# Token gather of a mixture-of-experts loop: the 0/1 matrix made the stationary operand, an eviction and transposes added, and the gather issued four weight chunks sooner

## What is computed

```python
def moe_swiglu(u, w_router, w_gate, w_up, w_down):
    logits = jnp.dot(t, w_router, preferred_element_type=jnp.float32)
    top_logit, top_idx = lax.top_k(logits, TOP_K)
    top_w = jax.nn.softmax(top_logit, axis=-1)
    gate = jnp.einsum('tk,tke->te', top_w, jax.nn.one_hot(top_idx, N_EXPERTS, ...)).astype(u.dtype)
    for e in range(N_EXPERTS):
        out = out + gate[:, e:e + 1] * swiglu(t, w_gate[e], w_up[e], w_down[e])
```

## Time and profile before

| | us |
|---|---|
| median of 3 runs | 1728.83 |
| lowest and highest | 1723.35, 1729.32 |
| the profiled execution's own time | 1729.09 |
| its span, from the first to the last instruction | 1727.3 |
| TensorE busy | 1595.1 |
| VectorE busy | 1303.5 |
| ScalarE busy | 1018.5 |

### The profile page before, as it was taken

One profiled execution on the slowest core, in us unless ns is written; L12 is line 12 of the kernel. 1 busy time (PEld: TensorE's weight loads), 2 busy tenths in 40 slices (PEclk: granted clock), 3 DMA queues, 4 the chain that ended last, 5 costly groups with the idle time before them and its releaser, 6 DMA issues.

```text
span 1727.3 us, 21466 instructions
## 1 busy us (share of the span) xinstructions
PE 1595.1 (92%) x8127; PEld 1346.3 (78%) x8127; DVE 1303.5 (75%) x1112; ACT 1018.5 (59%) x853; POOL 14.4 (1%) x35
## 2 busy tenths in 40 slices
PE   5996799998799777999999999999999999999985
PEld 5976688886697666888888888888888888888864
DVE  5986443544598654888988888888889888988863
ACT  4536243333454533767677767767677776777642
POOL 3000000000000000000000000000000000000000
PEclk9996799998899876999999999999999999999987
DMA  8430355553344033999999999999999999999930
GB/s 247 147 122 25 105 178 188 194 171 122 104 142 158 25 104 107 362 380 328 371 372 330 370 375 329 372 342 358 374 345 356 374 341 358 377 336 363 376 133 24
DMA packets 203166, 439.70 MB, mean 255 GB/s; under 512 B 12072, under 2 KB 31088, under 8 KB 203120
## 3 DMA queue, kind: packets, MB, share of 16 engines
q1 hardware_dynamic: 197040, 437.32, 71.7%
q10 hardware_dynamic: 6080, 1.74, 0.5%
HBM read 437.98 MB, written 1.05 MB: 254 GB/s over the span
## 4 chain that ended last, share of the span: by engine, by line
PE 85%; DVE 10%; ACT 3%; issue 1%; ACTq 0%; POOL 0%; DVEq 0%; POOLq 0%
PE bank L1177 25%; PE bank L1179 25%; PE bank L1178 25%; PE bank L1441 2%; DVE wlo L748 2%; PE bank L1472 1%; PE bank L1172 1%; PE bank L1247 1%; DVE uTl L798 1%; DVE scores L898 1%; PE bank L1311 1%; ACT work L497 1%; PE bank L1454 1%; PE bank L1455 1%; DVE work L793 0%
## 5 line engine op out<-in xcount | busy, mean ns | idle before, releaser
L748 DVE TENSOR_TENSOR wlo<-raw,whi 128x2048 fp32r<-128x2048 f32 x415 | 935.2, 2287 | 131.2 <-ACT whi L667 94.1
L667 ACT ACTIVATE whi<-raw 128x2048 fp32r<-128x2048 f32 x341 | 633.3, 1910 | 25.6 <-DMA raw<-in_w_exp_down_dram 14.4
L1177 PE MATMUL bank<-whi,uTh 128*128 128x512 f32 (+1 forms) x1312 | 520.9, 397 | 18.0 <-DVE uTl L798 17.0
L1179 PE MATMUL bank<-whi,uTl 128*128 128x512 f32 (+1 forms) x1312 | 513.3, 391 | 0.0
L1178 PE MATMUL bank<-wlo,uTh 128*128 128x512 f32 (+1 forms) x1312 | 512.8, 391 | 0.0
L1177 PEld LDWEIGHTS bank<-whi,uTh 128*128 128x128 f32 x1312 | 250.0, 191 | 70.4 <-DVE uTl L798 14.7
L1179 PEld LDWEIGHTS bank<-whi,uTl 128*128 128x128 f32 x1312 | 249.7, 190 | 52.8
L1178 PEld LDWEIGHTS bank<-wlo,uTh 128*128 128x128 f32 x1312 | 250.3, 191 | 49.5
L1177 PE MATMUL bank<-whi,hTr 128*128 128x512 f32 x552 | 218.1, 395 | 7.0 <-DVE hTr L964 4.4
L1178 PE MATMUL bank<-wlo,hTr 128*128 128x512 f32 x552 | 217.0, 393 | 0.0
L1179 PE MATMUL bank<-whi,hTr 128*128 128x512 f32 x552 | 216.8, 393 | 0.0
(11 more groups left out here) (212 smaller groups left out, 1158.2 us busy)
## 6 DMA issues: line engine op xcount, KB each, us to landing
raw<-in_w_exp_gate_dram SPq DMA_DIRECT2D x112, 1024.0 KB, 5.2
raw<-in_w_exp_up_dram SPq DMA_DIRECT2D x112, 1024.0 KB, 5.2
raw<-in_w_exp_down_dram SPq DMA_DIRECT2D x112, 1024.0 KB, 5.0
raw<-in_w_in_dram SPq DMA_DIRECT2D x28, 1024.0 KB, 5.4
raw<-in_w_ffn_gate_dram SPq DMA_DIRECT2D x11, 1024.0 KB, 5.0
raw<-in_w_ffn_up_dram SPq DMA_DIRECT2D x11, 1024.0 KB, 5.1
raw<-in_w_ffn_down_dram SPq DMA_DIRECT2D x11, 1024.0 KB, 4.8
raw<-in_w_out_dram SPq DMA_DIRECT2D x8, 1024.0 KB, 5.0
```

The source lines that it names most:

```text
L667: nc.scalar.activation(whi[:, s % SPLIT, :], raw[:, s % RAW, :], ACT.Copy).then_inc(hi_a, 1)
L748: return V.tensor_tensor(wlo[:, n % RAW, :], raw[:, n % RAW, :], whi[:, n % SPLIT, :].bitcast(F32), ALU.subtract).then_inc(lo_ready, 1)
L1177: T.matmul(o, sth, mvh, start=start, stop=False)
L1179: return T.matmul(o, stl, mvh, start=False, stop=stop)
```

## The change

The stationary operand of the gather becomes a tile of `sel`, the moving one 512 columns of the tokens' rows. High and low parts are added into the same bank, so that a bank holds 512 features of the 128 gathered tokens, places on partitions: 8 matmuls instead of 32, into banks 1 and 3. ScalarE evicts both banks to a new region `ug` (`tokens_out`). TensorE transposes `ug` in eight blocks of 128 into banks 7 and 1 (`gathered`), ScalarE copies the high parts from there, and VectorE, which before copied the low parts, now subtracts the high parts from the banks.

The order: the selection moves from chunk 35 to chunk 20, the gather matmuls from chunk 39 to chunk 35, with a wait for the hidden row of round 5. Behind chunk 39 stand the eight transposes and then the turn of round 6. Ahead of the loop, for the first item, the two parts follow each other.

```diff
+        ug = region(2560, D)
@@ ScalarE
+            def tokens_out(i, q):
+                act.wait_ge(gath, i * 2 + (q + 1))
+                nc.scalar.activation(ug[:, q * NC:(q + 1) * NC], bank(GATHER_BANKS[q]), ACT.Copy).then_inc(ug_ready, 1)
             def tokens_hi(i, q):
-                act.wait_ge(gath_hi, i * 2 + (q + 1))
-                nc.scalar.activation(uTeh[:, 4 * q:4 * q + 4, :], bank(GATHER_HI[q], 4, P), ACT.Copy).then_inc(euh_ready, 1)
+                act.wait_ge(gath_T, i * 2 + (q + 1))
+                nc.scalar.activation(uTeh[:, 4 * q:4 * q + 4, :], bank(TOKEN_BANKS[q], 4, P), ACT.Copy).then_inc(euh_ready, 1)
@@ ScalarE, in the loop, ahead of the weight copy of the chunk
+                    if n == GATHER_AT:
+                        for q in range(2):
+                            tokens_out(i + 1, q)
@@ VectorE
             def tokens_lo(i, q):
-                dve.wait_ge(gath_lo, i * 2 + (q + 1))
-                V.tensor_copy(uTel[:, 4 * q:4 * q + 4, :], bank(GATHER_LO[q], 4, P)).then_inc(eul_ready, 1)
+                s = slice(4 * q, 4 * q + 4)
+                dve.wait_ge(euh_ready, i * 2 + (q + 1))
+                V.tensor_tensor(uTel[:, s, :], bank(TOKEN_BANKS[q], 4, P), uTeh[:, s, :].bitcast(F32), ALU.subtract).then_inc(eul_ready, 1)
@@ TensorE
-            def gather(i, q, source, to, gathered):
+            def gather(i):
                 pe.wait_ge(sel_ready, i * 2 + 2)
-                for c in range(4):
+                for q in range(2):
                     for t in range(TT):
-                        k = 4 * q + c
-                        last = T.matmul(bank(to[q], 4, P)[:, c, :], source[:, t, k * P:(k + 1) * P], sel[:, t, :],
-                                        start=t == 0, stop=t == 1)
-                last.then_inc(gathered, 1)
+                        T.matmul(bank(GATHER_BANKS[q]), sel[:, t, :], unh[:, t, q * NC:(q + 1) * NC], start=t == 0, stop=False)
+                        last = T.matmul(bank(GATHER_BANKS[q]), sel[:, t, :], unl[:, t, q * NC:(q + 1) * NC], start=False, stop=t == 1)
+                    last.then_inc(gath, 1)
+            def gathered(i):
+                for q in range(2):
+                    pe.wait_ge(ug_ready, i * 2 + (q + 1))
+                    for c in range(4):
+                        last = T.transpose(bank(TOKEN_BANKS[q], 4, P)[:, c, :], ug[:, (4 * q + c) * P:(4 * q + c + 1) * P], ident[:, :])
+                    last.then_inc(gath_T, 1)
@@ TensorE, behind a chunk
                     if n == LAST_UP:
                         pe.wait_ge(comb_ready, i + 2)
-                        for q in range(2):
-                            gather(i + 1, q, unh, GATHER_HI, gath_hi)
+                        gathered(i + 1)
                         turn(r)
-                        for q in range(2):
-                            gather(i + 1, q, unl, GATHER_LO, gath_lo)
+                    if n == GATHER_AT:
+                        pe.wait_ge(exh_ready, i * EXR + (EXR - 1))
+                        gather(i + 1)
@@
-SELECT_AT = LAST_UP - 4
-GATHER_HI = [1, 7]
-GATHER_LO = [3, 0]
+SELECT_AT = 20
+GATHER_AT = LAST_UP - 4
+GATHER_BANKS = [1, 3]
+TOKEN_BANKS = [7, 1]
```

More of the change, by code:

```diff
@@ L318, in trunk @@
         rlog, rdiff, rexp, sel_count, ranks, table_ready = (sem(n) for n in ("rlog", "rdiff", "rexp", "sel_count", "ranks", "table_ready"))
-        sel_ready, gath_hi, gath_lo, euh_ready, eul_ready, comb_ps, comb_ready = (sem(n) for n in (
-            "sel_ready", "gath_hi", "gath_lo", "euh_ready", "eul_ready", "comb_ps", "comb_ready"))
+        sel_ready, gath, ug_ready, gath_T, euh_ready, eul_ready, comb_ps, comb_ready = (sem(n) for n in (
+            "sel_ready", "gath", "ug_ready", "gath_T", "euh_ready", "eul_ready", "comb_ps", "comb_ready"))
         exsil, exh_ready, exT_ps, exT_hi, exT_ready = (sem(n) for n in ("exsil", "exh_ready", "exT_ps", "exT_hi", "exT_ready"))
@@ L693, in _ @@
             for q in range(2):
+                tokens_out(0, q)
+            for q in range(2):
                 tokens_hi(0, q)
@@ L1457, in _ @@
             pe.wait_ge(unl_ready, TT)
-            for q in range(2):
-                gather(0, q, unh, GATHER_HI, gath_hi)
-            for q in range(2):
-                gather(0, q, unl, GATHER_LO, gath_lo)
+            gather(0)
+            gathered(0)
             with pe.Fori(0, n_items) as i:
```

## The result

| | before | after |
|---|---|---|
| median, us | 1726.33 (4 runs) | 1741.38 (4 runs) |
| lowest to highest | 1723.35 to 1729.32 | 1737.58 to 1744.53 |
| the profiled execution, its span | 1729.09, 1727.3 | 1737.58, 1735.8 |
| mean granted clock | 0.949 | 0.953 |

The ratio of the times is 1.0093, with a 95% interval from 1.0069 to 1.0117: the change makes the kernel 0.9% slower, about 15 us. The forecast was 1744, from 1736 to 1753.

A forecast was written before the change was run, and what follows sets the result against it. TensorE was taken to bound the expert loop. Eight item ends at +11.4 us, the first item at -1.0 and clock falls at +5.0 gave +15.4 on 1729.1 us: 1744, range 1736 to 1753.

The forecast's parts named there:

- The bound: Expert loop: TensorE, busy for all 983 us, sets the time, although the DMA engines have a share of 0.99.
- The work: TensorE per item: 3.5 us of gather removed, 1.86 of gather and 0.87 of transposes added; 0.75 us shorter by work alone.
- Chunk 35: Moved gather between two chunks: 1.86 us of uncovered TensorE time per item; hidden row then ready to start at T' + 0.57.
- T': Moment in the changed kernel when an item's last up chunk's matmuls are issued; forecast as 912.27 in the item shown.
- The item's end: After the last up chunk: TensorE idles 0.4, then 1.6 to 1.7 us; first down product 3.50 us on; item +1.43 us.
- First item: Gather ahead of the loop, at half clock: gains 1.4 us at most, some lost again; -1.0 us taken.
- longer time at half clock: Behind the first item's gather: expected to lose some of its gain of at most 1.4 us, leaving -1.0.
- The clock: Idle time at item ends lowers TensorE's granted clock: 0 to 8 falls, 0 to 13 us; three taken, +5.0 us.
- The price of one fall: Cost of one drop to half clock, read from eight matmuls taking 3.46 us instead of 1.81: 1.65 us.
- the second rival: Clock falls in every item, if transposes do not keep TensorE awake: +23.6 us, 1752.7; chance 0.14.
- VectorE in time: Item end: hidden row at T' + 0.2, turn follows transposes at once; +1.10 us per item, +7.8 in all, 1736.9; chance 0.11.
- Faster: Item-end stall is hidden and only the work counts: -7.0 us, 1722; chance 0.05.

The follow-up runs named there:

- the version with the other order: Changed kernel with round 6's up chunks ahead of round 5's down chunks, two turned-row buffers, transposes and last turn moved; ratio 0.9937, median 1716.26 us.
- The exchange of two lines in the kernel before: Kernel before with the sixteen low-part gather matmuls ahead of the last turn instead of behind it; ratio 1.0111.
- the filler: Changed kernel with seven extra 512-column matmuls behind an item's last turn, results overwritten; ratio 1.0038.
- the late transposes: Changed kernel with the eight transposes behind chunk 40 instead of ahead of the last turn; ratio 1.0201.
- 0.9 us more in each item: Changed kernel with four more 512-column matmuls behind chunk 12, results overwritten; ratio 1.0113.

## Why the prediction was right, and what was off

**The bound.** TensorE is the bound in the loop, and the DMA share of 0.99 was not a second one: the version with the other order went 0.8 us an item below the kernel before.

**The work.** 0.75 us less per item was forecast; the version without waits shows 0.8.

**Chunk 35.** The gather there took 1.8 us of TensorE, uncovered. The evictions stood at 0.90 and 1.81 behind the activation (forecast 0.96 and 1.87). The hidden row came at T' + 0.57, exactly the forecast.

**The item's end.** Turn at T' + 1.31 (1.29), eviction at 2.00 (2.08), subtraction at 2.63 (2.70), first product at 3.45 (3.50). TensorE's recorded idle time was 0.27 and 1.49 us, where 0.4 and 1.6 to 1.7 were forecast. The exchange of two lines in the kernel before shows the cause by itself, the filler shows that the time behind the turn is a wait, and the late transposes that the turn's start hangs on VectorE. Without a fall the item grew by 1.38 us (124.65 - 123.27), where 1.43 was forecast.

**First item: a term that was mis-sized.** From the first gather matmul to the first product it is 0.9 us less, where -1.0 was forecast. But the forecast took off "longer time at half clock" behind it, and the first products ran at full clock instead: 2.2 us more, -3.1 in all. This is in part luck. In one of the two further executions of the changed kernel the first products ran at half clock, as before, and the whole was -2.0.

**The clock: the term that was mis-sized.** "I take three, +5.0", the prediction says. No row gave that number; it was a pick between bounds of 0 and 8. It was seven in each of three profiles, 10.0 us. The price of one fall, 1.65, measured 1.6, but 0.4 at the last end. In the count this is close to the second rival, "the clock falls in every item", to which I gave 0.14. By the profile the loop itself is 18.9 us longer and not 16.4; it would be 21 without the 2.2 us of the first products. The item ends were not independent: in the changed kernel an item with a fall is 126.24 us long, and the next item end falls too. With 0.9 us more in each item two of eight fall, with a longer gap in items of 126.95 us two of eight, with items of 126.60 us three in a row and then three that hold. This points to the distance between the gaps as much as to the gap, but each of these three is one execution, so it is argued and not shown. Why the first end always holds and the second always falls in the changed kernel is not settled by these runs.

Loop and first item together are 18.0 us longer in the profiled executions (18.9 - 0.9), the medians differ by 15; the interval of the ratio, 12 to 20 us, holds both. That the median stands so near to 1744 is in part luck: the falls cost 5 us more than forecast, and the first item gave back 2 us more.

**The other rivals.** VectorE in time: no, 0.27 us of wait remain ahead of the turn. Faster: no; the amount of work does count, but only once the chain has other cover. The Trainium skill (TensorE: Matmul & The Clock Gate, "Why this matters for your kernels") asks for no gap above about 3 us; here a single wait of 1.49 us cost the clock at four of eight item ends, and even with the transposes ahead of it counted as idle the gap was 2.1 us (915.51 to 917.62). That its Part 4 does not count transposes as busy can be neither shown nor excluded from these runs: with the low-part gather ahead of the turn, four transposes and a wait were enough for a fall, and with twelve transposes around two waits the first item end held.

## What to carry to other kernels

Before you shorten or move work on the engine that sets the pace, ask which chain on the other engines runs under it, and measure that chain: here 1.7 us of matmuls covered the eviction and subtraction behind a turn, and saving 0.8 us of work cost 3 us an item. Then look for cover that must run anyway; putting a whole weight chunk behind each step of the chain turned the loss of 0.9% into a gain of 0.6%. If a short wait must stay, matmuls in it whose results nobody reads can pay for themselves through the clock: seven of them brought back more than half of the loss.

## What the runs showed of the hardware

- The granted clock can fall to half behind four transposes and a single wait of 1.49 us, with matmuls at full speed ahead of them. Half speed is there at the restart (a first product of 0.79 us, at 1044.22 in the kernel without cover) or begins a few matmuls later (in the changed kernel's last item end the first two take 0.49 us and the third 0.63). The same two waits (0.27 and 1.49 us) brought it down at seven of eight item ends in three executions, and at two of eight in the one execution with 0.9 us more in each item; that the distance between the waits decides is not shown.
- A wait of TensorE costs more than its recorded idle time. The item without waits is 122.45 us; with 1.76 us of idle time in two waits it is 124.65, so 0.22 us more for each wait. With 3.57 us in four waits it is 126.94, again 0.23 for each. A 512-column matmul's record is 0.39 us long and the next normally starts 0.23 us behind it; across a wait this overlap is lost, and the first one takes 0.49, which is about this size.
- A DMA share of 1.00, at 359 GB/s over 970 us, didn't mean that the loads set the pace: TensorE was busy throughout.
- Identical code ahead of the loop ended up to 9 us apart in different executions (654.3 to 663.7).
